# One key product for two attention heads, and a copy from the upper partitions

## What is computed

```python
def mla_project(c_q, c_kv, k_r, q_norm_g, kv_norm_g, w_uq, w_ukv, cos=None, sin=None):
    q = (rmsnorm(c_q, q_norm_g) @ w_uq).reshape(B, T, MLA_HEADS, MLA_QK)            # 8 heads x 96
    kv = (rmsnorm(c_kv, kv_norm_g) @ w_ukv).reshape(B, T, MLA_HEADS, MLA_NOPE + MLA_V)
    k_nope, v = kv[..., :MLA_NOPE], kv[..., MLA_NOPE:]                              # 64 and 64
    ...
def attend(q, k, v):
    s = jnp.einsum('bqhd,bkhd->bhqk', q, k) * MLA_SCALE
    return jnp.einsum('bhqk,bkhd->bqhd', jax.nn.softmax(s, axis=-1), v)
```

## Time and profile before

| | us |
|---|---|
| median of 3 runs | 2402.03 |
| lowest and highest run | 2399.49, 2406.5 |
| profiled execution | 2396.57 |
| its span | 2394.8 |
| TensorE busy in the span | 2128.6 (89%) |
| VectorE, ScalarE, GpSimd busy | 727.4, 490.0, 278.8 |
| attention stage of layer 0, of layer 1 | 161, 81 |

### The profile page before, as it was taken

The page is one execution under the profiler, slowest core; times in us unless marked ns, Lnnn a source line. Parts: engine busy times, 40 slices in busy tenths (PEclk is TensorE's granted clock), DMA queues, the critical chain, the costliest instruction groups (busy, mean ns, idle before and its releaser), DMA issues. The chain is left out here.

```text
span 2394.8 us, 53930 instructions
## 1 busy us (share of the span) xinstructions
PE 2128.6 (89%) x23930; PEld 1357.3 (57%) x23930; DVE 727.4 (30%) x1768; ACT 490.0 (20%) x1120; POOL 278.8 (12%) x463
## 2 busy tenths in 40 slices
PE   6999999899799999999999779998988899977784
PEld 2454444789644444446566464554888787744442
DVE  1023334777431011310100032445775311200001
ACT  2122322333130000301111132323332301100011
POOL 0000000444100001101111100001442000011111
PEclk8999999899999999999999989998999999989896
DMA  7149816000121312448999821210000345899993
GB/s 281 58 146 331 313 49 236 3 4 4 55 88 53 105 53 105 170 166 324 381 383 383 306 92 43 67 49 1 4 4 13 144 145 190 281 379 381 383 383 120
DMA packets 182915, 399.91 MB, mean 167 GB/s; under 512 B 6656, under 2 KB 29952, under 8 KB 182496
## 3 DMA queue, kind: packets, MB, share of 16 engines
q1 hardware_dynamic: 170528, 361.94, 42.0%
q0 software_dynamic: 8576, 23.08, 2.6%
q10 hardware_dynamic: 3648, 12.45, 1.8%
HBM read 365.47 MB, written 31.98 MB: 166 GB/s over the span
## 5 line engine op out<-in xcount | busy, mean ns | idle before, releaser
L481 PE MATMUL ps<-H,memory 128*128 128x512 f32 (+2 forms) x1728 | 616.7, 513 | 11.8 <-DMA memory<-in_w_in 10.0
L481 PEld LDWEIGHTS ps<-H,memory 128*128 128x128 f32 (+1 forms) x1728 | 328.8, 191 | 287.3 <-issue 251.3
L715 PE MATMUL ps<-memory 64*64 64x32 f32 (+2 forms) x10112 | 333.1, 230 | 42.9 <-DVE memory L1621 17.6
L978 PE MATMUL ps<-memory 128*32 128x256 f32 x5120 | 304.5, 400 | 60.2 <-DMA memory<-in_eu 58.6
L715 PEld LDWEIGHTS ps<-memory 64*64 64x64 f32 x10112 | 318.9, 143 | 53.9 <-DVE memory L1621 19.1
L481 PE MATMUL ps<-memory 128*128 128x512 f32 (+4 forms) x960 | 336.3, 500 | 8.3 <-issue 3.0
L978 PEld LDWEIGHTS ps<-memory 128*32 128x32 f32 x5120 | 192.0, 115 | 170.6 <-issue 89.8
L481 PEld LDWEIGHTS ps<-memory 128*128 128x128 f32 (+2 forms) x960 | 175.1, 185 | 159.1 <-issue 140.2
L1003 PE MATMUL ps<-memory 128*32 128x256 f32 x2560 | 144.8, 380 | 4.9 <-ACT memory L1324 3.8
L1892 POOL TENSOR_TENSOR memory<-memory,cons 128x256 f32<-128x256 f32 x160 | 120.3, 769 | 122.5 <-DVE memory L1577 93.0
L1956 POOL DMA_DIRECT2D expert_rows<-memory x128 | 69.3, 541 | 436.5 <-DVE memory L1825 412.6
(11 more groups left out here) (251 smaller groups left out, 1808.4 us busy)
## 6 DMA issues: line engine op xcount, KB each, us to landing
memory<-in_eg SPq DMA_DIRECT2D x32, 2048.0 KB, 19.0
memory<-in_eu SPq DMA_DIRECT2D x32, 2048.0 KB, 24.9
memory<-in_ed SPq DMA_DIRECT2D x32, 2048.0 KB, 21.6
memory<-in_w_ada SPq DMA_DIRECT2D x24, 2048.0 KB, 9.9
memory<-in_w_in SPq DMA_DIRECT2D x20, 2048.0 KB, 8.4
expert_rows<-memory SPq DMA_DIRECT2D x4, 3456.0 KB, 23.6
memory<-in_w_out SPq DMA_DIRECT2D x4, 2048.0 KB, 8.0
memory<-expert_rows ACTq DMA_DIRECT2D x19, 384.0 KB, 7.0
```

Of the source, the lines that this page charges most:

```text
L481: ins = mm(ps[0:M, bank, 0:w], lhs(k), rhs(k), start=(k == 0), stop=(k == n - 1))
L715: ins = mm(out[cols, j], lhs[rows, j, :], rhs[rows, j], start=(n == 0), stop=(n == len(terms) - 1))
L978: ins = mm(out_.rearrange("p (x n) -> p x n", x=2), XGT[:, k, g * GROUP:g * GROUP + GROUP], sets[b][:, 0:2, k * 512 + c * P:k * 512 + c * ...
```

## The change

The two key products of an even head take 128 weight columns instead of 64: the 64 of the even head and the 64 of the odd head beside them. The result fills all 128 partitions of bank 1. An odd head then has no key product; its `make` consists of the three query products, and `heads_made1` is signalled by the last of those. ScalarE's key copy reads partitions 0 to 63 of bank 1 for the even head and partitions 64 to 127 for the odd one, and writes partitions 0 to 63 of `Kh` both times. The weights are laid out to match: an even head's transfer is 128 rows of 544 floats (272 KB), an odd head's 128 rows of 288 floats (144 KB).

```diff
-HW = 3 * QK + 2 * NOPE
+HW = 3 * QK + 4 * NOPE
...
-                sp.dma_start(WH[:, h % 2, :], headw[l, h, :, :]).then_inc(sem(f"headw_loaded{h % 2}"), 16)
+                cols = 3 * QK if h % 2 else HW
+                sp.dma_start(WH[:, h % 2, 0:cols], headw[l, h, :, 0:cols]).then_inc(sem(f"headw_loaded{h % 2}"), 16)
...
-                    product(0, w, lambda k: WH[:, b, k * QK:k * QK + QK], lambda k: CQ[:, k, 0:w], 3, QK)
-                    product(1, T, lambda k: WH[:, b, 3 * QK + k * NOPE:3 * QK + k * NOPE + NOPE],
-                            lambda k: CKV[:, k, :], 2, NOPE).then_inc(sem(f"heads_made{b}"), 1)
+                    ins = product(0, w, lambda k: WH[:, b, k * QK:k * QK + QK], lambda k: CQ[:, k, 0:w], 3, QK)
+                    if b == 0:
+                        ins = product(1, T, lambda k: WH[:, b, 3 * QK + k * 2 * NOPE:3 * QK + (k + 1) * 2 * NOPE],
+                                      lambda k: CKV[:, k, :], 2, 2 * NOPE)
+                    ins.then_inc(sem(f"heads_made{b}"), 1)
...
-                    act.copy(Kh[0:NOPE, b, :], ps[0:NOPE, 1, :]).then_inc(sem("heads_copied"), 1)
+                    act.copy(Kh[0:NOPE, b, :], ps[NOPE * b:NOPE * b + NOPE, 1, :]).then_inc(sem("heads_copied"), 1)
...
-    uk = a["w_ukv"].reshape(L, 2, P, HEADS, NOPE + VD)[..., :NOPE].transpose(0, 3, 2, 1, 4).reshape(L, HEADS, P, 2 * NOPE)
+    uk = a["w_ukv"].reshape(L, 2, P, HEADS // 2, 2, NOPE + VD)[..., :NOPE].transpose(0, 3, 2, 1, 4, 5)
+    uk = np.repeat(uk.reshape(L, HEADS // 2, P, 4 * NOPE), 2, 1)
```

## The result

| us | before | changed |
|---|---|---|
| median of 4 runs | 2402.75 | 2380.08 |
| lowest and highest run | 2399.49, 2406.5 | 2373.93, 2388.1 |
| profiled execution | 2396.57 | 2388.1 |
| its span | 2394.8 | 2386.4 |

The ratio is 0.9889, with an interval of 0.9855 to 0.9923. The two profiled executions are only 8.5 us apart.

A forecast was written before the change was run, and what follows sets the result against it. TensorE's own instruction stream was taken to bound both attention stages. Removing odd heads' key products gave 6.9 us in layer 0 plus 6.1 in layer 1, all else nothing: 2402.0 - 13.0 = 2389.0 us, range 2382 to 2396.5.

The forecast's parts named there:

- the sum's end: Both attention stages: 6.9 us from layer 0 plus 6.1 from layer 1, 13.0 us, taken as the whole gain.
- nothing is given back there: Stages behind attention: first weights load during attention and later loads follow TensorE's progress, so no gain is lost.
- shifts of the clock in stages that the change doesn't touch: Untouched stages: small clock shifts counted inside the forecast's 78%, seen in earlier runs as a spread of 7 us.
- costed at nothing: Even heads' 128-column key loads: hidden beside the preceding product, so 0 us; 1.6 us over both layers if uncovered.
- the rivals: Layer 0 gain lost to transfers 4%, clock falling in layer 1 9%, crossing copy as new bound 4%, two-pass copy 5%.
- `in_w_ada` wait: Layer 0, L502: late adaLN weight groups turn the four 1.72 us into waits, giving 2395.9 us; 4%.
- clocks of 0.99 and 0.95 in the two stages: Clock rival: layer 1's odd heads lose clock, 1.5 us in each of four, 6 us gone, giving 2395; 9%.
- second group of copies of another length: Odd heads' crossing key copy takes longer: two passes, 2393.6 us, 5%; four passes, 2415 us, 4%.
- new wait for the probabilities: Layer 1 odd heads' transposes, L652: TensorE arrives before the first tile's probabilities and gives back 0.28 us.
- the wait of 0.56 us at L610 stays: Layer 0 odd heads, before `rotate`: key copy still ends about 0.6 us after the transposes, so this wait is unchanged.
- the sum of 6.9 us: Layer 0's odd heads: four heads at 1.72 us each, the whole price of the removed records showing.
- The other end of my price, 1.93: Upper price of an odd head's four removed records, 0.48 us each by group busy time, including each head's drain.

The follow-up runs named there:

- the two widened kernels: Kernel before with 128-column key products in even heads only, 2406.14 us, or in all heads with the odd copy crossing, 2402.41; no product removed.
- the three delays: One, two or three extra products before layer 1's recurrent input projection: on the changed kernel 2386.82, 2387.6, 2387.75 us; on the kernel before 2411.48, 2409.01, 2412.31.
- the copy without the crossing: Changed kernel with odd heads' key copy reading partitions 0 to 63, so odd heads use the even heads' keys: 2389.15 us.

## Why the prediction was wrong, and what in it was right

**The step that failed is the sum's end: that what the two attention stages give, 13.0 us, is all.** The prediction took "nothing is given back there" for everything behind the stages, and put shifts of the clock in stages that the change doesn't touch down as a spread around the forecast, a term of nothing in the mean. The runs showed a gain of 22.7 us by the first medians and 23.5 by means. The two stages hold 14.4 of it, 1.4 more than the sum, and nearly all of these 1.4 are the even heads, costed at nothing. Of the 9.1 us outside the stages some 6 go with a granted clock that is higher on average, 0.9462 instead of 0.9421. Why it is higher, and where the last 3 us lie, stays open. The parts follow, what was right first.

**The mechanism in the stages was right.** The stages are TensorE's own stream, and what left the stream shortened them. No wait for a transfer stands in the lists, the wide loads are hidden (a load starts every 0.43 us), the crossing copy takes 580 ns of itself, 32 records are gone, and none of the rivals came: no `in_w_ada` wait, clocks of 0.99 and 0.95 in the two stages, no second group of copies of another length. Of the odd heads of layer 1 even the detail holds. Two rows answer to the earlier trace rows:

```profile
1497.05 0.66 PE L655 MATMUL ps<-cons,memory 128*128 128x128 f32 x4 [0.35 <-DVE memory L1487]
...
1498.05 0.67 PE L613 MATMUL ps<-memory,cons 96*96 96x256 f32 x2 [0.34 <-ACT memory L1107]
```

There is the new wait for the probabilities (0.35 us, 0.28 forecast), the old one for the copies (0.34, about 0.35 forecast), and from `rotate` to `rotate` a head takes 7.56 us instead of 9.01: 1.45 less, as worked out.

**The price of a removed product came out by luck, with two errors that cancel.** I took 4 x 0.43 = 1.72 us for an odd head's removed records, and left the wait at L610 where it was. Measured in layer 0 are 1.95 us, of which 1.72 are the records and 0.23 the two switches of width that went with them. (With both products wide an odd head has 242.40 - 238.11 = 4.29 us from `make` to transposes, and 2.58 without them: 1.71 for the four records alone.) But the key copy starts later behind the transposes: 237.40 - 236.59 = 0.81 us now, 184.63 - 184.04 = 0.59 in the earlier trace rows. Half of that is the missing overlap of the crossing copy; the other half is that transposes without a switch in front of them start sooner after `make`, while the copies don't. Those 0.22 us are given back, and the result is 1.73 to 1.74 us. So "the wait of 0.56 us at L610 stays" was wrong, and so was a price without the switches; the sum of 6.9 us hides both. The other end of my price, 1.93, came from the busy time of the group, 30.9 us over 64 records. I had put its excess down to a drain that stays. The 1.95 us measured say that most of the excess goes, and that it is the switch is my reading.

**The even heads were costed at nothing and gain 0.15 us each.** I asked only whether the wider loads would be exposed. What I did not ask is what the width of the neighbours is. The even head loses its switches too, 0.24 us, and gives 0.10 of it back in front of `rotate` (220.50 - 219.18 = 1.32 us from the transposes, 185.26 - 184.04 = 1.22 in the earlier trace rows): 19.27 to 19.12 us. Eight heads make 1.2 us. With 4 x 1.74 + 4 x 0.15 = 7.6 us in layer 0 and 1.72 + 3 x 1.45 + 4 x 0.14 = 6.6 in layer 1 the sum is 14.2 us instead of 13.0. Measured over seven profiled executions with the full number of products (the two widened kernels and the three delays among them) and seven with the removal in both layers (three delays and the copy without the crossing among them), the stages' means are 160.6 and 152.7 us in layer 0, 77.6 and 71.1 in layer 1: 7.9 + 6.5 = 14.4 us, uncertain by 1.0. Without the two widened kernels, whose even heads have their gain already, it is 15.1.

**"Behind the stages nothing is given back" held, but more came than the stages give.** The runs gained 23.5 us by means and the two stages hold 14.4. In the same fourteen executions, less the added products, the span's mean goes from 2406.2 to 2387.4, which is 18.8 us: 14.4 in the two stages, 3.8 in layer 1's scan, 0.7 in all others. A span differs by some 5.6 us from run to run, so each mean of seven is uncertain by 2.1 us and their difference by 3; the 3.8 and the distance from 18.8 to 23.5 are 1.3 and 1.6 times that, so neither is clear of chance. Part of that distance is in the choice of executions: in all seven series with the removal in both layers the profiled one is slower than the mean of the others, 2389.8 us against 2385.2 over all. The difference of the runs is better known, since 95 and 16 of them give it to about 1.4 us, and the 9.1 us between 23.5 and 14.4 are far outside both uncertainties. What goes with it is the granted clock: its mean over an execution is 0.9421 before and 0.9462 after, and among the runs of the kernel before alone the time falls by 1.4 us for each 0.001 of it. Runs of equal clock (0.9425 to 0.9465) have means of 2403.7 us (32 runs) and 2386.8 (9 runs), which is 16.9 us, uncertain by 1.2. So about 14 us are shown in their place, some 6 go with a higher clock elsewhere (0.0041 at 1.4 us for each 0.001), and 3 are placed by neither. Why the changed kernel gets the clock isn't shown, nor is it shown that the clock is the cause and not a companion of the shorter time. The start of the scan was one candidate and fell as far as it was tried; which stages hold the gain in the timed runs stays open, because those leave no rows.

**The base was low.** I added the 13.0 to a median of three runs, 2402.0. The mean of 95 is 2407.5. From there the same sum would have given 2394.5, further from the 2383.9 than the forecast was: the low base hid half of the miss. "A spread of 7 us" was read off three runs; one kernel's runs reach from 2392.73 to 2418.22.

## What to carry to other kernels

When a product of few columns stands between wide ones, count what lies around it as well as its records: taking it out or making it as wide as its neighbours is worth the two switches, here 0.24 us. After a stage has been shortened, look at the wait that then ends last and ask whether its engine needs all that it waits for; splitting one wait gave 11.5 us by means on top of the change's 23.5, some 7.5 of them in the waits themselves. And put the forecast on a base of many runs with their clock, since three runs may lie 5 us to one side.

## What the runs showed of the hardware

- A switch between products of 64 weight columns and ones of 96 or 128 keeps the next weight load from running ahead: 0.94 us from load to load instead of 0.43, and 0.24 us of TensorE's time for a pair of switches.
- ScalarE's copies from PSUM overlap by 0.1 us when they follow each other (starts 0.47 to 0.49 us apart at 0.58 us each). If one reads from partition 64 and writes to 0 while its neighbours read from partition 0, the starts are 0.60 and 0.61 apart.
- In a scan with the same 5400 or so records of TensorE, the mean granted clock came out between 0.84 and 0.93 and the length between 197 and 212 us. The long end is a kernel whose scan is untouched, both products wide:

```profile
1660.00:1872.00 212.00, 191.34 (x5431) 184.34 (x5428) 136.41 (x351) 63.48 (x197) 76.47 (x107) 0.84 0.03 7
```
